# Head sums of a hybrid decoder block: two one-pass products with a 0/1 matrix, of a rounded part and its rest, in the place of full-precision products and turns; another order of the first loads

## The reference

```python
kk = (k * k_k).reshape(B, T, H, N)
kk = kk / jnp.maximum(jnp.linalg.norm(kk, axis=-1, keepdims=True), 1e-12)
k = k * (1.0 + (a - 1.0) * k_a)
y = rwkv7_scan(r, decay, k, v, kk, a)            # a sequential scan over the positions
...                                              # head norm of y, gain and bias
bonus = jnp.sum(rh * kh * r_k, axis=-1, keepdims=True) * vh
y = y + bonus.reshape(B, T, RWKV_WIDTH)
return y * jax.nn.silu(g)
```

## Time and profile before

| | us |
|---|---|
| median of 3 runs | 1893.8 (1893.34 to 1894.69) |
| the profiled execution's own time | 1894.24 |
| its span in the trace | 1892.5 |
| TensorE busy | 1863.2 (98%) |
| VectorE busy | 1171.7 (62%) |
| ScalarE busy | 771.7 (41%) |
| GpSimd busy | 456.8 (24%) |

### The profile page before, as it was taken

The page is one execution under the profiler, slowest core; times in us unless marked ns, Lnnn a source line. Parts: engine busy times, 40 slices in busy tenths (PEclk is TensorE's granted clock), DMA queues, the critical chain, the costliest instruction groups (busy, mean ns, idle before and its releaser), DMA issues.

```text
span 1892.5 us, 38318 instructions
## 1 busy us (share of the span) xinstructions
PE 1863.2 (98%) x15168; PEld 1509.3 (80%) x15168; DVE 1171.7 (62%) x2238; ACT 771.7 (41%) x1545; POOL 456.8 (24%) x1096
## 2 busy tenths in 40 slices
PE   8999999999999999999999999999999999999996
PEld 5878888888888887888888888888888778878885
DVE  5666576766667577666766667575757754346433
ACT  6444434343434345434343434343434443243221
POOL 0005041322314150041423324150505051101110
PEclk9999999999999999999999999999999999999998
DMA  5533332333333335332323333333333543465543
GB/s 179 173 109 90 88 99 79 99 87 87 90 92 94 87 89 174 106 93 78 98 84 92 88 93 88 89 93 88 92 84 100 165 126 108 128 205 167 156 126 124
DMA packets 194962, 207.70 MB, mean 110 GB/s; under 512 B 98272, under 2 KB 101472, under 8 KB 194784
## 3 DMA queue, kind: packets, MB, share of 16 engines
q1 hardware_dynamic: 194784, 205.26, 37.5%
HBM read 183.18 MB, written 22.02 MB: 108 GB/s over the span
## 4 chain that ended last, share of the span: by engine, by line
PE 93%; DVE 3%; POOL 1%; DMA 1%; ACT 1%; issue 1%; SPq 0%; DVEq 0%; ACTq 0%; POOLq 0%
PE psum L1153 75%; PE psum L1138 3%; PE psum L1287 2%; PE psum L1222 2%; PE psum L1260 1%; PE psum L1438 1%; PE psum L1321 1%; PE psum L1402 1%; PE psum L1206 1%; PE psum L1409 1%; PE psum L1247 1%; PE psum L1177 1%; PE psum L1162 1%; PE psum L1192 1%; PE psum L1391 1%
## 5 line engine op out<-in xcount | busy, mean ns | idle before, releaser
L1153 PE MATMUL psum<-x_hi,w_hi 128*128 128x512 f32 x2144 | 883.9, 412 | 10.2 <-DVE x_lo L741 7.7
L1153 PE MATMUL psum<-x_hi,w_lo 128*128 128x512 f32 x2144 | 837.7, 391 | 0.0
L1153 PE MATMUL psum<-x_lo,w_hi 128*128 128x512 f32 x2144 | 837.4, 391 | 0.0
L732 DVE TENSOR_TENSOR w_lo<-w_raw,w_hi 128x512 fp32r<-128x512 f32 x536 | 379.9, 710 | 607.6 <-ACT w_hi L539 587.5
L539 ACT ACTIVATE w_hi<-w_raw 128x512 fp32r<-128x512 f32 x536 | 335.4, 629 | 816.1 <-PE psum L1153 799.6
L1153 PEld LDWEIGHTS psum<-x_hi,w_hi 128*128 128x128 f32 x2144 | 403.2, 188 | 112.7 <-DVE w_lo L732 17.5
L1153 PEld LDWEIGHTS psum<-x_hi,w_lo 128*128 128x128 f32 x2144 | 402.7, 188 | 88.8
L1153 PEld LDWEIGHTS psum<-x_lo,w_hi 128*128 128x128 f32 x2144 | 404.0, 188 | 79.4 <-issue 7.2
L495 POOL TENSOR_TENSOR sub_t<-sub_l,sub_io 128x60 f32<-128x60 f32 (+24 forms) x496 | 189.2, 381 | 879.0 <-DMA sub_l<-scratch_L 841.4
L497 POOL TENSOR_TENSOR sub_io<-sub_io,sub_t 128x60 f32<-128x60 f32 (+24 forms) x496 | 191.6, 386 | 38.9
L516 POOL TENSOR_TENSOR v<-v,kb 128x512 f32<-128x512 f32 x29 | 38.4, 1325 | 268.7 <-ACT kb L678 268.3
(11 more groups left out here) (236 smaller groups left out, 1786.3 us busy)
## 6 DMA issues: line engine op xcount, KB each, us to landing
w_raw<-in_w_in SPq DMA_DIRECT2D x408, 256.0 KB, 2.7
w_raw<-in_w_out SPq DMA_DIRECT2D x128, 256.0 KB, 2.7
sub_l<-scratch_L SPq DMA_DIRECT2D x16, 512.0 KB, 4.7
stage<-in_x_t SPq DMA_DIRECT2D x20, 256.0 KB, 3.4
stage<-scratch_MIX SPq DMA_DIRECT2D x19, 256.0 KB, 4.1
scratch_MIX<-sa SPq DMA_DIRECT2D x16, 256.0 KB, 3.2
scratch_MIX<-ym SPq DMA_DIRECT2D x16, 256.0 KB, 3.2
lora<-in_x_t SPq DMA_DIRECT2D x16, 256.0 KB, 2.9
```

What stands on the lines that cost most here:

```text
L732: nc.vector.tensor_tensor(w_lo[gq % SPLIT][:], w_raw[gq % RAW][:], w_hi[gq % SPLIT][:].bitcast(F32), ALU.subtract).then_inc(w_ready, 1)
L1153: mm = nc.tensor.matmul(psum[:, s % 2], wt[gq % SPLIT][:, cols], xx[:, c], start=(c == 0 and wt is w_hi and xx is x_hi), stop=(c == KC - 1 ...
```

## The change

The squares and the bonus terms are rounded to float32r by ScalarE, VectorE makes the rest, and TensorE multiplies both with a rounded 0/1 matrix `heads_r` into one PSUM bank: two one-pass products of 128x512, in which the sum of a head stands in each of its 64 rows. Max and reciprocal are then taken on 512 columns, in step 14. Steps move: the norm products from 10 and 12 to 9, the use of kk from 13 to 14, the shift of v from 14 to 15, that of r from 21 to 20, the bonus terms from 22 to 21. New waits guard buffers now used twice (the rounded tiles lie on kkt, zs and wr). The mean squares' second staging buffers move to `late`. In the start the first weights and activations are loaded ahead of `par1`.

```diff
+        def with_rounded(name, shape):
+            offset = nc.sbuf_base
+            return sb(name, shape), nc.alloc_sbuf_tensor_at(name + "_r", [P, HALF], F32R, offset=offset)
...
-        second = [z[:].rearrange("p m d -> p (m d)") for z in (wr, kkt, zs)]
+        second = [late[:, i] for i in range(SECOND)]
... # SyncE, start
+                load_w(0)
+                load_x(0, 0)
                 sp.dma_start(par1[:], io["par1"]).then_inc(par1_landed, 16)
-                load_w(0)
-                for c in range(2):
-                    load_x(0, c)
+                load_x(0, 1)
                 sp.dma_start(cst[:], io["consts"]).then_inc(consts_landed, 16)
... # ScalarE
                     if at == 5:
                         act.wait_ge(k_ready, j + 1)
-                        nc.scalar.activation(s1, k, ACT.Square, scale=p(n, "k_k")).then_inc(squares, 1)
+                        if j >= 2:
+                            act.wait_ge(u_full, 2 * (j - 1))
+                        nc.scalar.activation(s1, k, ACT.Square, scale=p(n, "k_k"))
+                        nc.scalar.activation(kkt_r[:], k, ACT.Square, scale=p(n, "k_k")).then_inc(squares, 1)
+                    if at == 22:
+                        act.wait_ge(rkr_ready, j + 1)
+                        copy(zs_r[:], s1).then_inc(rkr_high, 1)
...
                 act.wait_ge(inited, 1)
-                act.wait_ge(par1_landed, 16)
+                copy(part[:, 0:2], eps[:])
                 for part_ in range(4):
                     high(part_)
+                    if part_ == 0:
+                        act.wait_ge(par1_landed, 16)
                     slices(0, part_)
... # VectorE
-                    if at == 14:
+                    if at == 15:
                         shift(v[:], p(n, "mu_v"))
-                    if at == 11:
-                        dve.wait_ge(norm_done, 2 * j + 1)
-                        then(nc.vector.tensor_scalar(inv2[:], psum[:, 2, 0:BH], 1e-24, None, ALU.max))
-                        then(nc.vector.reciprocal(inv2[:], inv2[:]))
-                        then(nc.vector.tensor_copy(grow.rearrange("p (m d) -> p m d", d=HD),
-                                                   inv2[:].unsqueeze(2).broadcast_to([P, BH, HD])))
+                    if at == 6:
+                        dve.wait_ge(squares, j + 1)
+                        then(nc.vector.tensor_tensor(wr_r[:], s1, kkt_r[:].bitcast(F32), ALU.subtract))
+                        dve.sem_inc(squares_split, 1)
+                    if at == 14:
+                        dve.wait_ge(norm_done, j + 1)
+                        then(nc.vector.tensor_scalar(grow, psum[:, 3], 1e-24, None, ALU.max))
                         dve.sem_inc(inv_ready, 1)
-                    if at == 13:
-                        dve.wait_ge(norm_done, 2 * j + 2)
-                        then(nc.vector.scalar_tensor_tensor(k, k, p(n, "k_k"), psum[:, 3], ALU.mult, ALU.mult))
+                        then(nc.vector.reciprocal(grow, grow))
+                        dve.wait_ge(kkt_full, j)
+                        then(nc.vector.scalar_tensor_tensor(k, k, p(n, "k_k"), grow, ALU.mult, ALU.mult))
                         dve.sem_inc(kk_read, 1)
...
-                    if at == (17 if last_of_half(j) else 21):
+                    if at == (17 if last_of_half(j) else 20):
                         shift(r, p(n, "mu_r"))
+                    if at == 23:
+                        dve.wait_ge(rkr_high, j + 1)
+                        then(nc.vector.tensor_tensor(kkt_r[:], s1, zs_r[:].bitcast(F32), ALU.subtract))
+                        dve.sem_inc(rkr_split, 1)
-                    if at == 22:
+                    if at == 21:
                         then(nc.vector.tensor_tensor(
                             qr[:, :, 0:4:3], r.rearrange(chunks, b=NB, c=2),
... # TensorE
-                    if at == 10:
-                        pe.wait_ge(squares, j + 1)
-                        ...
-                        for b in range(NB):
-                            mm = nc.tensor.matmul(psum[:, 2, 2 * b:2 * b + 2], s1[:, b * P:(b + 1) * P],
-                                                  const("head_of"), start=True, stop=True)
-                        mm.then_inc(norm_done, 1)
-                    if at == 12:
-                        pe.wait_ge(inv_ready, j + 1)
+                    if at == 9:
+                        pe.wait_ge(squares_split, j + 1)
                         pe.wait_ge(sigma_a, j + 1)
+                        pe.wait_ge(z_read, j)
                         if j % PAIRS == 0:
                             pe.wait_ge(va_read, j // PAIRS + 1)
-                        for b in range(NB):
-                            mm = turn(psum[:, 3, b * P:(b + 1) * P], grow[:, b * P:(b + 1) * P])
-                        mm.then_inc(norm_done, 1)
+                        nc.tensor.matmul(psum[:, 3], heads_r[:], kkt_r[:], start=True, stop=False)
+                        nc.tensor.matmul(psum[:, 3], heads_r[:], wr_r[:], start=False, stop=True
+                                         ).then_inc(norm_done, 1)
                     if at == 24:
-                        pe.wait_ge(rkr_ready, j + 1)
-                        pe.wait_ge(kk_read, j + 1)
-                        nc.tensor.matmul(psum[:, 3], const("same_head"), s1, start=True, stop=True
+                        pe.wait_ge(rkr_split, j + 1)
+                        pe.wait_ge(inv_ready, j + 1)
+                        nc.tensor.matmul(psum[:, 3], heads_r[:], zs_r[:], start=True, stop=False)
+                        nc.tensor.matmul(psum[:, 3], heads_r[:], kkt_r[:], start=False, stop=True
                                          ).then_inc(bonus_done, 1)
```

More of the change, by code:

```diff
@@ L74 @@
 for _name, _w in (("ident", 128), ("same_head", 128), ("mean", 128), ("amask", 256), ("dist", 192),
-                  ("dist0", 192), ("head_of", 2)):
+                  ("dist0", 192)):
     CONSTS[_name] = (_at, _at + _w)
@@ L93, in constants @@
     t["dist0"] = np.where((d >= 0) & (d < BT) & (key + r - r % SB >= BT), d, 1e33)
-    t["head_of"] = (r // HD == np.arange(2)[None, :])
     return np.concatenate([t[n].astype(np.float32) for n in CONSTS], axis=1)
@@ L186, in program @@
         lora_up = [sb(f"lora_up{i}", [P, P]) for i in range(2)]
-        inv2 = sb("inv2", [P, BH])
+        heads_r = sb("heads_r", [P, P], F32R)
         pc = sb("pc", [P, 2, NCH])
@@ L210, in program @@
         uv = late[:, 6:8].rearrange("p c (b h d) -> p c b h d", b=NB, h=2)
-        kkt = sb("kkt", [P, BH, C])
+        kkt, kkt_r = with_rounded("kkt", [P, BH, C])
         sub_l = sb("sub_l", [P, SUB, SUB])
@@ L218, in program @@
         ym = sb("ym", [P, BH, C])
-        zs = sb("zs", [P, BH, C])
-        wr = sb("wr", [P, BH, C])
+        zs, zs_r = with_rounded("zs", [P, BH, C])
+        wr, wr_r = with_rounded("wr", [P, BH, C])
         score = sb("score", [P, 4, 2 * BT])
@@ L273, in program @@
         k_ready, squares, norm_done, inv_ready = sem("k_ready"), sem("squares"), sem("norm_done"), sem("inv_ready")
+        squares_split, rkr_high, rkr_split = sem("squares_split"), sem("rkr_high"), sem("rkr_split")
         kk_read, rkr_ready, bonus_done, bonus_read = (sem("kk_read"), sem("rkr_ready"), sem("bonus_done"),
@@ L644, in recurrence @@
                         act.wait_ge(kkt_full, i + 1)
+                        if i < INTERVALS - 1:
+                            act.wait_ge(norm_done, i + 2)
                         copy(kkt[:].rearrange("p m d -> p (m d)"), psum[:, 7]).then_inc(kkt_read, 1)
@@ L653, in recurrence @@
                         act.wait_ge(y_centred, i + 1)
+                        if i < INTERVALS - 1:
+                            act.wait_ge(bonus_done, i + 2)
                         nc.scalar.activation(ysq[:], ym[:], ACT.Square).then_inc(y_squared, 1)
@@ L1087, in _ @@
                 dve.sem_inc(inited, 1)
-                dve.wait_ge(par1_landed, 16)
                 for part_ in range(4):
                     low(part_)
+                    if part_ == 0:
+                        dve.wait_ge(par1_landed, 16)
                     slices(0, part_)
@@ L1094, in _ @@
                 dve.wait_ge(sinks_landed, 16)
+                nc.vector.tensor_copy(heads_r[:], const("same_head"))
                 then(nc.vector.tensor_scalar(neg_sinks[:], sinks[:], -1.0, None, ALU.mult))
@@ L1172, in channels @@
                         pe.wait_ge(bonus_read, j)
-                        if j == PAIRS:
-                            pe.wait_ge(yt_read, PAIRS - 1)
+                        if j >= 3:
+                            pe.wait_ge(yt_read, PAIRS - 1 if j == PAIRS else j - 2)
                         for x in range(2):
```

3 lines of the change are left out of this document (removed).

## The result

| | before | changed kernel |
|---|---|---|
| median of 20 runs beside each other, us | 1894.15 (1892.35 to 1896.67) | 1897.36 (1895.93 to 1900.29) |
| ratio | | 1.0018 (95%: 1.0012 to 1.0025) |
| profiled execution, us | 1894.24 | 1896.58 |
| span, us | 1892.5 | 1894.8 |

I had said 1889.1. The time lies in the range of 1877 to 1900, but the sign is the other one: 3.2 us lost where 4.7 were to be gained. The effect lies inside the 0.2% that I had called unmeasurable, but with 20 runs of each the interval excludes "no change".

A forecast was written before the change was run, and what follows sets the result against it. TensorE, 98% busy, bounds the kernel until it meets late VectorE values. Pairs 1 to 15 -3.3, pair 0 -1.3, start -1.3, pairs 7 and 15 +1.2: -4.7 us, 1889.1 against the median; range 1877 to 1900.

The forecast's parts named there:

- TensorE's own gain: TensorE alone, norm sums 0.90, inverse-norm turns 0.45, bonus 0.88, less 0.92 added: 1.31 us a pair, 21.0 over 16 pairs.
- Step 13: Turned softmax block: TensorE arrives earlier and waits 0.50 us for VectorE's last scaling, leaving 0.44 of the gains.
- "worth nothing" of step 12: Removing the inverse-norm turns saves TensorE 0.45 us, but it then waits for VectorE's scaling, so nothing is gained.
- Steps 14 to 17: The 128x512 reciprocal in VectorE's queue delays TensorE's corner product to 457.35, 0.2 us a pair later than before.
- the eleven pieces: VectorE's chain from 447.10 to the corner product, w_lo through first inverse level and handover to TensorE: 10.12 us.
- Pair 0, with no softmax behind it: -1.3: First pair of heads, without attention and recurrence beside it: 1.3 us gained.
- Start -1.3: First weights and activations issued ahead of the parameters: 1.3 us gained (bounds 0 and 1.7), limited by the constants' landing.
- Pairs 7 and 15: +1.2: ScalarE's rounding copy delays the state copy TensorE's chain awaits: 0.6 us lost in each pair, 1.2 in all.
- ScalarE's 0.6: Loss in each of pairs 7 and 15 from the bonus rounding copy standing ahead of the state copy on ScalarE.
- Step 24: Bonus product falls from 0.88 to 0.46 us, its operand's trip through VectorE and ScalarE hidden: 0.42 gained a pair.
- rival C: GpSimd's copies fall into both VectorE chains up to step 17: pair +0.48 us, time 1899.6, slower; chance 0.21.

## Why the prediction was wrong

- **TensorE's own gain**: right. In the version with the norm products in step 12 the differences between steps 9 and 11 fall by 0.92 (0.90 forecast), a whole regular pair by about 1.1 of the 1.31.
- **Step 13**: right in mechanism and nearly in size, wait 0.60 in pair 4 and 0.53 on average for 0.50. (I called the turns of step 12 eight instructions; the row says four. The price of 0.45 came from starts and doesn't hang on it.) The "worth nothing" of step 12 was right for the order as it was, and the norm products in step 12 show it: put work there and it is free.
- **"Steps 14 to 17"**: the failed step. The mechanism (reciprocal of 3.35 in one queue, corner late) was right and without the reciprocals the kernel is 12.9 us faster than before. The term, the corner 0.20 later than in the kernel before, was too small: measured in pair 4's own frame it is 0.49 (0.40, and the pair stood 0.09 early from step 3 on). Of the 0.29, 0.14 came in with the scaling that runs beside GpSimd's copy, and about 0.15 are the sum: the eleven pieces added to 10.41 where I had 10.12 and 0.13 of reserve; the maximum took 0.83 for 0.75, kk 0.90 for 0.78, attention 0.56 for 0.50. Each is small; all have the same sign, as a follower starts later than its forerunner's busy time: the maximum lasts 0.68 and the next starts after 0.83. For kk the kernel before had it too (the row below this list). Over 13 regular pairs the 0.29 and the 0.05 behind step 17 make most of the 4.5 us between forecast and measurement.
- **"Pair 0, with no softmax behind it: -1.3"** and **"Start -1.3"**: together -0.41 for -2.6. I had put the reciprocal behind step 17 at nothing, as the w_lo of later quarters are made three steps ahead. In pair 0 the mean product is not so covered: it waits 1.25 for VectorE, pair 0 loses 1.52 there, and without the reciprocals, or with the shift of v in step 18, it loses 0.01 or 0.02 and pair 0 gains 1.1 in all. The 0.52 before the bonus product I hadn't looked for either. What the start is worth no run settles.
- **"Pairs 7 and 15: +1.2"**: +2.9 in all for +0.8 with their regular part. ScalarE's 0.6 was there (0.56 and 0.47). The PSUM bank that VectorE empties late (0.39 and 0.44) and a corner that waits 1.31 in pair 15 were not in the sum.
- **Step 24**: right, a pair 0.42 shorter with the bonus alone in most pairs, 0.39 at that step in the whole. That the bonus also takes away a wait of 1.2 in the last stage was not in the sum: without this unforeseen gain the time would have been another 1.3 further from the forecast.

The row of kk in the kernel before (VectorE, pair 4), 0.75 busy; its follower starts at 447.49, 0.89 later, where I had added 0.78:

```profile
446.60 0.75 DVE L851 SCALAR_TENSOR_TENSOR work<-work,par,psum 128x512 f32<-128x512 f32 x1
```

The forecast was a difference of terms of 0.4 to 0.9 us a pair; 0.35 to 0.4 a pair more, with pair 0, was enough to turn its sign. That the time still lies in the range says little for the sum: the upper end was drawn for rival C. What I did not draw from my own working: the chain to step 17 stood with no slack left, so any addition there goes one to one into the time, and then the likely error has one side only. Rival C had the right direction and a share of the right mechanism; a pair +0.13 long, instead of its +0.48.

Left open: why the two versions with the shift in step 11 spread over 5.2 and 5.8 us in 5 runs each, where the changed kernel spreads over 4.4 and the kernel before over 4.3 in 20; why the transposed DMA of step 16 is late in single pairs of the version with the shift in step 13.

## What to carry to other kernels

Work taken off the busiest engine counts only until the next value from another queue: before you price an edit, list for each product that needs another engine the slack between that engine's end and the product's start, and let the edit draw on the smallest. An instruction that grows in an in-order queue is paid by whatever stands behind it there; the reciprocal of 8 columns took 0.20 in the kernel before, that of 512 takes 3.35:

```profile
437.44 0.20 DVE L845 RECIPROCAL inv<-inv 128x8 f32<-128x8 f32 x1
```

So ask what may pass in front: here a shift of 1.5 us moved two steps up, and 0.46 us of products moved into a wait, turned 3 us lost into 15 gained. And when a wait is taken away, look at the next one behind it: in pairs 7 and 15 it only moved from step 23 to step 24. When a chain has no slack, round its sum up, not to the middle.

## What the hardware showed that I had not expected

- GpSimd and VectorE stretch each other by whole instructions: GpSimd products of 0.25 and 0.26 lasted 0.73 and 0.72 beside VectorE instructions of 0.69 and 0.75, the four scalings 1.43 and 1.48 beside a copy, 1.01 without. So it matters which of GpSimd's steps a VectorE instruction falls into: the shift in step 18 and that in step 11 differ by about 5 us.
- A reciprocal on 128x512 takes 3.35, a maximum or a product on as many elements 0.68.
- The first product's start varies from 6.35 to 9.20 between the profiled kernels, and not by the order of the loads alone: with the same order the first weights landed at 4.12 in the kernel before and at 5.67 in the version with the bonus alone.
